# Second block's heads: granules split ahead of x's low halves, token sums dealt among query matmuls, turns among compressed keys

## The chip, the core and the metric

The kernel runs on one core of a Trainium2 chip. The metric is the device time of one execution in microseconds. The core has five engines that run their own instruction queues and meet at semaphores: TensorE (PE, with its weight loads PEld), VectorE (DVE), ScalarE (ACT), GpSimd (POOL) and SyncE (SP), which issues the transfers.

## What is computed

Two blocks of two layers each act on x, 512 tokens by 1024 features, in fp32. The first block (a gated MLP, a retention and a delta-rule branch) isn't touched by the change. The second block reads, cut to what matters:

```python
x = rms_norm(x, final_norm_g)                # final norm of the first block
mem_n = _rmsnorm(mem, mem_norm)              # 256 memory rows
for i in range(2):
    h = _rmsnorm(x, norm_mix[i])
    proj = h @ w_in[i]                       # i = 0: c_q (384), c_kv (256), k_pe (64), q_mem (512)
    mix = mla(proj) if i == 0 else gqa(proj)
    kv = mem_n @ w_mem_kv[i]                 # memory keys and values
    k = _rmsnorm(kv[:, :, 0], memk_norm)
    mem_out = attention(_rmsnorm(q_mem), k, kv[:, :, 1])
    x = x + concat(mix, mem_out) @ w_out[i]
    x = x + swiglu(_rmsnorm(x, norm_ffn[i]))
```

In mla, c_q and c_kv ("compressed" queries, keys and values) are normalised per token and multiplied by further weights. A norm needs a sum of squares over features for each token.

## The kernel before

**Products in three passes.** Each fp32 product is three reduced-precision ones (`three`, L838 to L841): high x high, low x high, high x low. So activations and weights each exist as a high part (a rounding cast on ScalarE) and a low part (a subtraction on GpSimd; for some on VectorE). Weights come in granules of 128 x 1024 through four slots: SyncE loads `raw`, ScalarE casts `wh` (`hi2`), GpSimd subtracts into `wl` (`lo2`, `split`, L2405, two halves of 512 columns). `hi2(g)` and `lo2(g)` treat the granule four places behind g: `split_granules("mk", [3])` makes the low half of the fourth granule of mv. A slot is cast anew when TensorE has finished the granule in it.

**Groups.** `attention_plan` lists the dense products at a layer's head. Layer 0: mk (memory keys, 4 granules), cq (queries with the shared key kpe, 448 columns, 4), mv (memory values, 4), ckv (compressed keys, 256 columns, 2), qm (memory queries, 4), and so on. Layer 1: mk, mv, qm, kv and so on. `dense` runs a group: all granules but the last two go granule by granule over the tiles of 128 tokens; the last two go tile by tile, so that tiles finish one after the other. With `mix`, one turn stands behind each tile.

**Turns.** `turn` transposes a finished, normalised tile back (L1437) into bank 6 or 7 in alternation, and ScalarE (`feature`, L2168) takes it out; for cq and ckv VectorE also takes a low part from the bank (`lows`, L3147). A bank is free when both have been.

**Statistics.** `statistics` on TensorE sums squares over the partitions, with ones as a one-column moving operand (`token_sums`, L843 to L849): two transposes of gains (L1474), then sums of msum (memory, 2 columns), in layer 0 also of ssum and of the last square (4 each), and of ssb (4), which VectorE adds up from eight squares made on ScalarE (`square_b` L2069, `add_b` L3139). The signal "summed" starts VectorE's and ScalarE's roots, with which GpSimd scales the tokens (`scale_tokens`, L2571).

**Layer 1's x.** VectorE makes ht (`scale_x`, L3132) in four buffers, ScalarE casts it to hh (`scaled_hi`, L2061), GpSimd makes hl = ht - hh (`scaled_lo`, L2552) and so frees the buffer: ht of k = 4 waits for hl of k = 0. VectorE's own order there is scale_x 0..3, add_b 1, scale_x 4, 5, add_b 2, scale_x 6, add_b 3, scale_x 7, add_b 4..7. ScalarE's is:

```python
cast("mk", [0, 1]); scaled_hi(0..1); cast("mk", [2]); scaled_hi(2..3); square_b(0..1)
cast("mk", [3]); take(to_token, "mk"); square_b(2); scaled_hi(4); cast("mv", [0])
scaled_hi(5); square_b(3); scaled_hi(6..7); cast("mv", [1]); square_b(4..7)
memory_values(); cast("mv", [2, 3]); take_root("mx"), ...
```

All orders are written out by hand; each engine takes its queue strictly in that order.

Of the kernel before, what the change touches and what calls it, by code (L numbers as in the profile page):

```python
# [22 lines left out]
P = 128  # L23
# [3 lines left out]
NT = T // P  # L27
# [266 lines left out]
N2_ADDED = {0: 0, 2: 7, 3: 13, 4: 20}  # L294
# [56 lines left out]
X0_TURN = 9  # L351
QUERY_TURNS = ((("qA", 0), ("qA", 1)), (("qA", 2), ("qA", 3)), (("qpe0", 0), ("qpe0", 1)), ())
QB_TURNS = (4, 6, 8, 9)
FILL_STEPS = (0, 1, 2, 3, 4, 6, 8, 10, 12, 14, 16, 18)


# [97 lines left out]
def build(nc, stream, params, consts, consts2, gains, xin, memin, out, n_granules):  # L454
# [43 lines left out]
    mv = sb("mv", [P, 4, 2])  # L498
# [120 lines left out]
    for i in range(2):  # L619
        def tiles_at(n, count, at, shape=(P, T), dt=F32):  # L620
            return [sb(f"{n}_{i}_{t}", list(shape), dt, at=at + t * int(np.prod(shape[1:])) * 4) for t in range(count)]
        b = BUF[i]
# [110 lines left out]
    def bc(ap, shape):  # L733
        return ap.broadcast_to(shape)
# [7 lines left out]
    with block:  # L742
# [92 lines left out]
        def _(pe):  # L835
# [7 lines left out]
            def token_sums(o, sq, one, start, stop):  # L843

                w = one.shape[1]
                for t in range(sq.shape[1] // P):
                    m = mm(o[:, t * w:(t + 1) * w], sq[:, t * P:(t + 1) * P], one, start=start and t == 0, stop=stop,  # L849
                           skip_group_check=True)  # L850
                return m
# [485 lines left out]
            def attention_block(i):  # L1337
                b, t = BUF[i], t2[i]
                done = []

                def dense(name, parts, free, mix=None):

                    grp = GROUPS[i][name]
                    hi_, lo_ = {"h": (hh, hl), "m": (b["mh"], b["ml"]), "cq": (b.get("cqh"), b.get("cql")),
                                "ckv": (b.get("ckvh"), b.get("ckvl"))}[grp.src]
                    if grp.src == "m":
                        pe.wait_ge(ms["lo"].sem, ms["lo"].at(i + 1, 2))
                    if grp.src in ("cq", "ckv"):
                        turns = count_before(TURNS[i], grp.src) + dict(TURNS[i])[grp.src]
                        pe.wait_ge(t["feat"].sem, t["feat"].at(turns))  # L1350
                        pe.wait_ge(t["feat_lo"].sem, t["feat_lo"].at(3 if grp.src == "cq" else 5))
                    n = len(grp.granules)

                    def piece(q, x):

                        g = ATT0[i] + grp.g0 + q
                        w = g % SLOTS
                        pe.wait_ge(lo_ready, g + 1)
                        if q == 0:
                            free(x)  # L1360
                        for k, at in grp.granules[q]:
                            if grp.src == "h" and x == 0:
                                if i == 0:
                                    pe.wait_ge(s["xl_ready"].sem, s["xl_ready"].at(DEPTH, k + 1))
                                else:
                                    pe.wait_ge(n2["lo"], N2_SCALED[3] + k + 1)
                            r = slice(x * P, (x + 1) * P)
                            o = three(bk[grp.banks[x]][:, 0:grp.width], hi_[:, k, r], lo_[:, k, r],
                                      wh[w][:, at:at + grp.width], wl[w][:, at:at + grp.width], k == 0, k == grp.nk - 1)
                        if q == n - 1 and x < grp.tiles - 1:  # L1370
                            o.then_inc(t["tile_done"].sem, 1)
                        if x == grp.tiles - 1:
                            o.then_inc(granule_done, 1)

                    if parts == "tile":
                        return piece
                    for q in parts:
                        if q < n - 2:
                            for x in range(grp.tiles):
                                piece(q, x)  # L1380
                    if n - 1 in parts:
                        for x in range(grp.tiles):
                            for q in range(max(0, n - 2), n):
                                piece(q, x)
                            if mix and x < len(mix):
                                for a in mix[x] if name == "qB" and i == 0 else [mix[x]]:
                                    turn(*a)

                def whole(name, free, mix=None):
                    dense(name, range(len(GROUPS[i][name].granules)), free, mix)  # L1390
# [7 lines left out]
                def evacuated(name):  # L1398
                    return lambda x: taken(name, x)
# [64 lines left out]
                def turn_all(name):  # L1464
                    for a in turns(name):
                        turn(*a)

                def statistics():

                    pe.wait_ge(n2["added"], N2_ADDED[3 * i] + 7)  # L1470
                    keys = ("q_pe", "k_pe") if i == 0 else ("gqa_q", "gqa_k")
                    for x, key in enumerate(keys):
                        g = gain[:, GAIN[key]:GAIN[key] + 1]
                        nc.tensor.transpose(bk[7][:, (x + 1) * P:(x + 2) * P], bc(g, [P, P]), C2["ident"])  # L1474
                    pe.wait_ge(ms["red"].sem, ms["red"].at(i + 1, 1))
                    token_sums(bk[7], b["msum"][:, :], C2["ones"][:, 0:1], True, True)
                    if i == 0:
                        pe.wait_ge(s["sq_added"].sem, s["sq_added"].at(DEPTH, 6))
                        token_sums(bk[7][:, 384:], ssum[:, :], C2["ones"][:, 0:1], True, False)
                        pe.wait_ge(s["sq_ready"].sem, s["sq_ready"].at(DEPTH, 8))  # L1480
                        token_sums(bk[7][:, 384:], sq2[3][:, :], C2["ones"][:, 0:1], False, True)
                    token_sums(bk[7][:, 392:], ssb[:, :], C2["ones"][:, 0:1], True, True).then_inc(n2["summed"], 1)

                def fill_bank(tiles, before):

# [2 lines left out]

                if i == 0:
                    whole("mk", merged_taken)  # L1490
                    dense("cq", range(2), x_taken)
                    statistics()
                    dense("cq", range(2, 4), None)
                    whole("mv", evacuated("mk"))
                    turn_all("mk")
                    turn_all("cq")
                    whole("ckv", evacuated("cq"))
                    turn_all("kpe")
                    dense("qm", range(1), evacuated("ckv"))
                    pe.wait_ge(t["rr"].sem, t["rr"].at(root_index(i, "x0") + 1))  # L1500
# [20 lines left out]
                else:  # L1521
                    whole("mk", down_taken(4))
                    whole("mv", down_taken(0))
                    down_taken(7)(0)
                    statistics()
                    dense("qm", range(2), lambda x: taken("mv", x) if x < 2 else down_taken(0)(x))
                    dense("qm", range(2, 4), None, turns("mk"))
                    dense("kv", range(2), evacuated("qm"))
# [203 lines left out]
        def _(act):  # L1732
# [321 lines left out]
            def attention_block(i):  # L2054
# [115 lines left out]
                def features(name):  # L2170
                    for x in range(dict(TURNS[i])[name]):
                        feature(name, x)
# [8 lines left out]
                if i == 0:  # L2181
# [16 lines left out]
                    take_root("cq")  # L2198
                    memory_values()
                    features("mk")  # L2200
                    features("cq")
                    cast("mv", [2, 3])
                    take(to_token, "ckv")
                    features("kpe")
                    cast("ckv", [0, 1])
                    take_root("ckv")
# [193 lines left out]
        def _(pool):  # L2400
# [141 lines left out]
            def attention_block(i):  # L2542
# [30 lines left out]
                if i == 0:  # L2573
                    split_granules("mk", range(4))
                    split_granules("cq", range(4))
                    scale_tokens("mk")
                    scale_tokens("cq")
                    split_granules("mv", range(4))
                    split_granules("ckv", [0])
                    scale_tokens("ckv")  # L2580
                    split_granules("ckv", [1])
                    split_granules("qm", range(4))
                    split_granules("kA", [0])
                    scale_tokens("kA")
                    for name in ("vA", "kB"):
                        split_granules(name, [0])
                    scale_tokens("kB")
                    split_granules("vB", [0])
                    split_granules("qpe", [0, 1])
                    scale_tokens("qpe0")  # L2590
                    scale_tokens("qpe1")
                    split_granules("qA", [0, 1])
                    split_granules("qB", [0, 1])
                else:
                    split_granules("mk", [0, 1, 2])
                    for k in range(4):
                        scaled_lo(k)
                    split_granules("mk", [3])
                    split_granules("mv", [0])
                    for k in range(4, KD):  # L2600
                        scaled_lo(k)
                    split_granules("mv", [1, 2, 3])
                    scale_tokens("mk")
                    split_granules("qm", range(4))
                    split_granules("kv", range(4))
                    scale_tokens("kv")
                    split_granules("qA", range(4))
                    split_granules("qB", range(4))
# [934 lines left out]
```

## Time and profile before

| | us |
|---|---|
| median of 3 runs | 2619.16 (2618.93 to 2619.23) |
| profiled execution, whole | 2619.03 |
| its span, first to last instruction | 2617.2 |
| PE busy | 2560.6 (98%) |
| DVE busy | 1035.6 (40%) |
| ACT busy | 1070.2 (41%) |
| POOL busy | 1327.5 (51%) |
| mean granted TensorE clock | 0.995 |

Rows name the engine, the line of the kernel, the operation and its tiles; in a timeline the first number is the start and the second the duration, both in us from the start of the span, and a bracket gives the idle time before it and what ended it. Matmuls are pipelined: their spacing counts, not their duration. Layer 0's head lies from 1257 to 1360 us, layer 1's from 1959 to 2060.

### The profile page before, as it was taken

How to read it: one execution, taken by the hardware profiler on the slowest of the kernel's cores; microseconds unless marked ns; L12 is line 12 of the kernel's file. 1: busy time of each engine (PE TensorE's matmuls, PEld its weight loads, DVE VectorE, ACT ScalarE, POOL GpSimd, SP SyncE). 2: the span in 40 equal slices, each digit the busy share in tenths (PEclk: the TensorE clock that was granted, in tenths of full speed). 3: DMA queues.
4: the chain of work that ended last, by engine and by line, in shares of the span. 5: the costliest groups of instructions: out<-in, count | busy, mean ns of one | idle time of the engine just before them, and what ended most of it. 6: DMA issues, size and time to landing. Idle time of an engine off the chain costs nothing.

```text
span 2617.2 us, 36454 instructions
## 1 busy us (share of the span) xinstructions
PE 2560.6 (98%) x12788; PEld 2053.4 (78%) x12788; DVE 1035.6 (40%) x2185; ACT 1070.2 (41%) x1648; POOL 1327.5 (51%) x1016
## 2 busy tenths in 40 slices
PE   9999999999999999999999999999999989999999
PEld 7878878888778787888876468888887746888887
DVE  6567442115575653113656632111015584211100
ACT  6336443334526444323546433333234463333321
POOL 6424655567633665556652125666557212566653
PEclk9999999999999999999999999999999999999999
DMA  5212112323221211333331113323333101233332
GB/s 197 83 48 82 48 34 89 96 98 130 81 65 65 66 41 57 97 96 113 105 97 33 33 42 96 96 96 96 96 106 119 57 25 49 90 96 98 96 103 72
DMA packets 62360, 215.03 MB, mean 82 GB/s; under 512 B 7312, under 2 KB 10512, under 8 KB 61840
## 3 DMA queue, kind: packets, MB, share of 16 engines
q1 hardware_dynamic: 62224, 213.28, 25.6%
q8 instruction: 78, 1.28, 0.2%
q14 instruction: 58, 0.48, 0.1%
HBM read 211.16 MB, written 2.10 MB: 81 GB/s over the span
## 4 chain that ended last, share of the span: by engine, by line
PE 62%; DVE 3%; ACT 1%; issue 1%; POOL 0%; DVEq 0%; ACTq 0%
PE bank L839 16%; PE bank L841 16%; PE bank L840 16%; PE pair L1624 2%; PE pair L839 2%; PE pair L840 1%; PE pair L841 1%; PE bank L1583 1%; PE bank L1584 1%; PE bank L1606 1%; PE pair L1437 1%; DVE soft L3326 1%; PE pair L849 0%; PE bank L1581 0%; PE bank L1199 0%
## 5 line engine op out<-in xcount | busy, mean ns | idle before, releaser
L2405 POOL TENSOR_TENSOR wl<-raw,wh 128x512 fp32r<-128x512 f32 x766 | 1021.7, 1357 | 1163.3 <-ACT wh L2036 381.9
L839 PE MATMUL bank<-hh,wh 128*128 128x512 f32 x1584 | 624.7, 394 | 2.3 <-DVE y L2907 2.3
L841 PE MATMUL bank<-hh,wl 128*128 128x512 f32 x1584 | 616.9, 389 | 0.0
L840 PE MATMUL bank<-hl,wh 128*128 128x512 f32 x1584 | 616.6, 389 | 0.0
L839 PEld LDWEIGHTS bank<-hh,wh 128*128 128x128 f32 x1584 | 297.5, 188 | 62.9 <-issue 3.2
L841 PEld LDWEIGHTS bank<-hh,wl 128*128 128x128 f32 x1584 | 297.3, 188 | 62.6
L840 PEld LDWEIGHTS bank<-hl,wh 128*128 128x128 f32 x1584 | 297.6, 188 | 59.9 <-issue 0.5
L2356 ACT CAST wh<-raw 128x1024 fp32r<-128x1024 f32 x120 | 125.5, 1048 | 254.0 <-PE pair L841 140.2
L1794 ACT CAST wh<-raw 128x1024 fp32r<-128x1024 f32 x104 | 109.1, 1050 | 128.8 <-PE bank L841 96.1
L839 PE MATMUL bank<-wh,hh 128*128 128x512 f32 (+2 forms) x352 | 139.8, 397 | 2.7 <-ACT vg L1813 1.6
L2036 ACT CAST wh<-raw 128x1024 fp32r<-128x1024 f32 x84 | 86.9, 1048 | 127.0 <-PE bank L841 107.6
L841 PE MATMUL bank<-wh,hl 128*128 128x512 f32 (+2 forms) x352 | 134.1, 381 | 0.0
L840 PE MATMUL bank<-wl,hh 128*128 128x512 f32 (+2 forms) x352 | 134.0, 381 | 0.0
L2995 DVE TENSOR_TENSOR gs<-gs,bank 128x512 f32<-128x512 f32 x24 | 16.4, 684 | 286.3 <-PE bank L841 286.3
L3369 DVE TENSOR_TENSOR at<-row,bank 128x512 f32<-128x512 f32 x44 | 30.3, 688 | 202.2 <-PE bank L841 199.4
L1989 ACT CAST wh<-raw 128x1024 fp32r<-128x1024 f32 x72 | 75.2, 1045 | 85.1 <-PE pair L841 43.8
L839 PE MATMUL bank<-ah,wh 128*128 (+1 forms) x264 | 102.7, 389 | 0.0
L840 PE MATMUL bank<-al,wh 128*128 (+1 forms) x264 | 102.7, 389 | 0.0
L841 PE MATMUL bank<-ah,wl 128*128 (+1 forms) x264 | 102.7, 389 | 0.0
L2005 ACT ACTIVATE gs<-bank 128x512 f32<-128x512 f32 x48 | 28.8, 600 | 166.5 <-PE bank L841 166.5
L3366 DVE TENSOR_TENSOR at<-row,bank 128x512 f32<-128x512 f32 x44 | 30.3, 688 | 162.7 <-PE bank L841 162.1
L839 PEld LDWEIGHTS bank<-wh,hh 128*128 128x128 f32 x352 | 66.9, 190 | 16.6 <-ACT vg L1813 3.5
(466 smaller groups left out, 4695.6 us busy)
## 6 DMA issues: line engine op xcount, KB each, us to landing
raw<-stream SPq DMA_DIRECT2D x384, 512.0 KB, 3.5
mraw<-memin SPq DMA_DIRECT2D x3, 1024.0 KB, 6.1
par<-params SPq DMA_DIRECT2D x2, 1124.5 KB, 8.7
out<-xT SPq DMA_DIRECT2D x8, 256.0 KB, 2.0
con<-consts SPq DMA_DIRECT2D x1, 1540.0 KB, 15.1
xT<-xin SPq DMA_DIRECT2D x2, 512.0 KB, 4.8
xT<-xin SPq DMA_DIRECT2D x1, 1024.0 KB, 8.6
con<-consts SPq DMA_DIRECT2D x1, 512.0 KB, 3.0
```

The lines of the kernel that those rows point to most:

```text
L839: mm(o, ah, bh, start=start, stop=False)
L840: mm(o, ah, bl, start=False, stop=False)
L841: return mm(o, al, bh, start=False, stop=stop)
L1624: x = mm(bk[value_bank(i, phase, a)], vv, pts[a % 2][kb][:, :], start=(kb == 0), stop=(kb == nk - 1))
L1794: nc.scalar.copy(wh[g % SLOTS][:, :], raw[g % SLOTS][:, :]).then_inc(hi_ready, 1)
L1989: nc.scalar.copy(wh[g % SLOTS][:, :], raw[g % SLOTS][:, :]).then_inc(hi_ready, 1)
L2005: A(gs[e][:, :], bk[e], ACT.Sigmoid).then_inc(s["gate_taken"].sem, 1)
L2036: nc.scalar.copy(wh[g % SLOTS][:, :], raw[g % SLOTS][:, :]).then_inc(hi_ready, 1)
L2356: nc.scalar.copy(wh[slot][:, :], raw[slot][:, :]).then_inc(hi_ready, 1)
L2405: m = TT(wl[slot][:, c], raw[slot][:, c], wh[slot][:, c].bitcast(F32), ALU.subtract)
L3366: V.tensor_tensor(at_[j][:, :], row[:, :], bk[2 * j], ALU.mult).then_inc(t["f_gate"].sem, 1)
L3369: V.tensor_tensor(at_[j][:, :], row[:, :], bk[2 * j + 1], ALU.mult).then_inc(t["f_up"].sem, 1)
```

## The change

It has three parts. (1) In layer 0 the token sums become a generator, and two of its one-column steps follow each k of cq's second granule; the wait for ssb moves behind the other sums. (2) In layer 0 the three turns of cq stand behind ckv's tiles 0 to 2 in place of standing ahead of ckv; ScalarE's order follows. (3) In layer 1 GpSimd splits mk's fourth part before any low half of x, mv's first part after two of them and mv's second after four.

```diff
+CKV_TURNS = ((("cq", 0),), (("cq", 1),), (("cq", 2),), ())
...
-                def dense(name, parts, free, mix=None):
+                def dense(name, parts, free, mix=None, weave=()):
...
                             o = three(bk[grp.banks[x]][:, 0:grp.width], hi_[:, k, r], lo_[:, k, r],
                                       wh[w][:, at:at + grp.width], wl[w][:, at:at + grp.width], k == 0, k == grp.nk - 1)
+                            for _ in zip(range(2), weave):
+                                pass
...
-                                for a in mix[x] if name == "qB" and i == 0 else [mix[x]]:
+                                for a in mix[x] if name in ("ckv", "qB") and i == 0 else [mix[x]]:
...
+                def column_sums(o, sq, start, stop):
+
+                    for c in range(sq.shape[1] // P):
+                        yield mm(o[:, c:c + 1], sq[:, c * P:(c + 1) * P], C2["ones"][:, 0:1], start=start and c == 0, stop=stop,
+                                 skip_group_check=True)
...
                 def statistics():
 
-                    pe.wait_ge(n2["added"], N2_ADDED[3 * i] + 7)
+                    if i:
+                        pe.wait_ge(n2["added"], N2_ADDED[3 * i] + 7)
...
-                        token_sums(bk[7][:, 384:], sq2[3][:, :], C2["ones"][:, 0:1], False, True)
-                    token_sums(bk[7][:, 392:], ssb[:, :], C2["ones"][:, 0:1], True, True).then_inc(n2["summed"], 1)
+                        yield from column_sums(bk[7][:, 384:], sq2[3][:, :], False, True)
+                        pe.wait_ge(n2["added"], N2_ADDED[0] + 7)
+                    m = None
+                    for m in column_sums(bk[7][:, 392:], ssb[:, :], True, True):
+                        if m is not None:
+                            yield m
+                    m.then_inc(n2["summed"], 1)
...
                     whole("mk", merged_taken)
-                    dense("cq", range(2), x_taken)
-                    statistics()
+                    dense("cq", range(1), x_taken)
+                    sums = statistics()
+                    dense("cq", range(1, 2), None, None, sums)
+                    for _ in sums:
+                        pass
                     dense("cq", range(2, 4), None)
                     whole("mv", evacuated("mk"))
                     turn_all("mk")
-                    turn_all("cq")
-                    whole("ckv", evacuated("cq"))
+                    whole("ckv", evacuated("cq"), CKV_TURNS)
...
                     features("mk")
-                    features("cq")
                     cast("mv", [2, 3])
-                    take(to_token, "ckv")
+                    for x in range(NT):
+                        to_token("ckv", x)
+                        for a in CKV_TURNS[x]:
+                            feature(*a)
...
-                    split_granules("mk", [0, 1, 2])
-                    for k in range(4):
+                    split_granules("mk", range(4))
+                    for k in range(2):
                         scaled_lo(k)
-                    split_granules("mk", [3])
                     split_granules("mv", [0])
+                    for k in range(2, 4):
+                        scaled_lo(k)
+                    split_granules("mv", [1])
                     for k in range(4, KD):
                         scaled_lo(k)
-                    split_granules("mv", [1, 2, 3])
+                    split_granules("mv", [2, 3])
```

## Rows read from the trace of the kernel before

**Rows 1.** Part 1 of the page: busy time by engine.
```profile
PE 2560.6 (98%) x12788; PEld 2053.4 (78%) x12788; DVE 1035.6 (40%) x2185; ACT 1070.2 (41%) x1648; POOL 1327.5 (51%) x1016
```
**Rows 2.** Timeline of PE, layer 1's mv and token sums.
```profile
1977.16 0.39 PE L841 MATMUL bank<-wh,ml 128*128 128x512 f32 x1
1981.12 0.80 PE L839 MATMUL bank<-wh,mh 128*128 128x512 f32 x1 [3.56 <-POOL wl L2405]
1981.71 0.63 PE L840 MATMUL bank<-wl,mh 128*128 128x512 f32 x1
...
1986.72 0.38 PE L1474 MATMUL pair<-con,gain 128*128 128x128 f32 x2
...
1988.20 0.49 PE L839 MATMUL bank<-wh,hh 128*128 128x512 f32 x1
```
**Rows 3.** Timeline of POOL, layer 1: low halves of x (hl) and splits (wl).
```profile
1973.12 5.48 POOL L2552 TENSOR_TENSOR hl<-ht,hh 128x512 fp32r<-128x512 f32 x4
1978.57 4.97 POOL L2405 TENSOR_TENSOR wl<-raw,wh 128x512 fp32r<-128x512 f32 x4
1983.51 5.01 POOL L2552 TENSOR_TENSOR hl<-ht,hh 128x512 fp32r<-128x512 f32 x4
```
**Rows 4.** Timeline of ACT, layer 1: casts and squares.
```profile
1972.53 1.03 ACT L2036 CAST wh<-raw 128x1024 fp32r<-128x1024 f32 x1
...
1975.75 0.62 ACT L2061 CAST hh<-ht 128x512 fp32r<-128x512 f32 x1 [0.69 <-DVE ht L3132]
1976.28 1.05 ACT L2036 CAST wh<-raw 128x1024 fp32r<-128x1024 f32 x1
...
1980.31 1.04 ACT L2036 CAST wh<-raw 128x1024 fp32r<-128x1024 f32 x1
1981.26 2.19 ACT L2069 ACTIVATE sqb<-xT 128x512 f32<-128x512 f32 x4
```
**Rows 5.** Busy time by stretch: span, PE, PEld, DVE, ACT, POOL, granted clock, DMA.
```profile
1277.50:1281.00 3.50, 3.50 (x30) 3.36 (x28) 0.00 (x0) 2.17 (x2) 2.53 (x3) 1.00 0.73 190
1281.00:1287.00 6.00, 6.00 (x21) 5.52 (x21) 4.03 (x32) 0.36 (x2) 1.42 (x2) 0.50 0.43 153
1304.90:1308.30 3.40, 2.49 (x15) 1.64 (x14) 1.76 (x2) 2.03 (x5) 3.40 (x4) 1.00 0.01 5
1308.30:1311.70 3.40, 2.18 (x19) 1.97 (x20) 1.41 (x2) 1.94 (x4) 3.40 (x4) 1.00 0.18 42
...
1981.00:1983.00 2.00, 1.89 (x5) 1.50 (x6) 0.98 (x2) 2.00 (x5) 2.00 (x3) 0.50 0.44 78
```
**Rows 6.** Timeline of PE, layer 0: token sums and cq.
```profile
1278.56 0.38 PE L1474 MATMUL pair<-con,gain 128*128 128x128 f32 x2
...
1280.93 1.82 PE L849 MATMUL pair<-con,ssb 128*128 128x1 f32 x8
1282.60 0.72 PE L839 MATMUL bank<-wh,hh 128*128 128x448 f32 x1
...
1287.90 0.36 PE L841 MATMUL bank<-wh,hl 128*128 128x448 f32 x1
...
1294.79 0.40 PE L839 MATMUL bank<-wh,mh 128*128 128x512 f32 x1
```
**Rows 7.** Timeline of PE, layer 0: turns and ckv's start.
```profile
1305.91 0.60 PE L1437 MATMUL pair<-con,tok 128*128 128x128 f32 x4
...
1308.22 1.06 PE L1437 MATMUL pair<-con,tok 128*128 128x128 f32 x8 [0.29 <-ACT mk L2168]
1310.50 0.63 PE L1437 MATMUL pair<-con,tok 128*128 128x128 f32 x4 [1.22 <-DVE cql L3147]
1310.89 0.36 PE L839 MATMUL bank<-wh,hh 128*128 128x256 f32 x1
...
1312.39 0.38 PE L839 MATMUL bank<-wh,hh 128*128 128x256 f32 x1
```
**Rows 8.** Timeline of POOL, layer 0: ckv's two splits.
```profile
1307.34 4.99 POOL L2405 TENSOR_TENSOR wl<-raw,wh 128x512 fp32r<-128x512 f32 x4
```
**Rows 9.** Timeline of PE, layer 1: mk's turns among qm's tiles.
```profile
2003.21 0.44 PE L1437 MATMUL pair<-con,tok 128*128 128x128 f32 x2 [1.11 <-POOL tok L2571]
...
2006.26 0.38 PE L1437 MATMUL pair<-con,tok 128*128 128x128 f32 x2
2006.40 0.48 PE L839 MATMUL bank<-wh,hh 128*128 128x512 f32 x1
2006.71 0.39 PE L840 MATMUL bank<-wl,hh 128*128 128x512 f32 x1
```
**Rows 10.** Timeline of DVE, layer 1: ht of k = 4 and ssb.
```profile
1974.97 0.75 DVE L3132 SCALAR_TENSOR_TENSOR ht<-xT,gain,pair 128x512 f32<-128x512 f32 x1 [1.25 <-POOL hl L2552]
...
1984.33 0.69 DVE L3139 TENSOR_TENSOR ssb<-pair,sqb 128x512 f32<-128x512 f32 x1
```

More of the change, by code:

```diff
@@ L1473, in statistics @@
                         g = gain[:, GAIN[key]:GAIN[key] + 1]
-                        nc.tensor.transpose(bk[7][:, (x + 1) * P:(x + 2) * P], bc(g, [P, P]), C2["ident"])
+                        yield nc.tensor.transpose(bk[7][:, (x + 1) * P:(x + 2) * P], bc(g, [P, P]), C2["ident"])
                     pe.wait_ge(ms["red"].sem, ms["red"].at(i + 1, 1))
-                    token_sums(bk[7], b["msum"][:, :], C2["ones"][:, 0:1], True, True)
+                    yield from column_sums(bk[7], b["msum"][:, :], True, True)
                     if i == 0:
                         pe.wait_ge(s["sq_added"].sem, s["sq_added"].at(DEPTH, 6))
-                        token_sums(bk[7][:, 384:], ssum[:, :], C2["ones"][:, 0:1], True, False)
+                        yield from column_sums(bk[7][:, 384:], ssum[:, :], True, False)
                         pe.wait_ge(s["sq_ready"].sem, s["sq_ready"].at(DEPTH, 8))
-                        token_sums(bk[7][:, 384:], sq2[3][:, :], C2["ones"][:, 0:1], False, True)
-                    token_sums(bk[7][:, 392:], ssb[:, :], C2["ones"][:, 0:1], True, True).then_inc(n2["summed"], 1)
+                        yield from column_sums(bk[7][:, 384:], sq2[3][:, :], False, True)
[5 more added lines that the diff above has]
+                    m.then_inc(n2["summed"], 1)
                 def fill_bank(tiles, before):
@@ L1524, in attention_block @@
                     down_taken(7)(0)
-                    statistics()
+                    for _ in statistics():
+                        pass
                     dense("qm", range(2), lambda x: taken("mv", x) if x < 2 else down_taken(0)(x))
```

## Prediction

> **What bounds the kernel now.** I read the page first: TensorE is busy 98% of the span [rows 1], so time can come only from its few holes, from stretches at a lower clock and from its own instructions. Then I read the timeline of TensorE at the head of each of the second block's two layers, where the change lies, and the other engines' timelines there.
>
> Second layer: matmuls start 0.227 us apart; after the one at 1977.16 the next starts at 1981.12, having waited 3.56 us for GpSimd's low half of a weight granule [rows 2]. It is the last granule of mv (mk's four splits each serve the granule four places on, so "mk 3" is mv's last). GpSimd splits it from 1978.57 to 1981.09, behind four low halves of x that began at 1973.12 [rows 3], though its high half was cast by 1973.56 [rows 4]. The engine comes back at 0.43 us a matmul, the clock granted at 0.50 in that stretch [rows 2, 5]. The sums over tokens run from 1986.72 to 1988.20 [rows 2].
>
> First layer: the token sums are one cluster of 2 transposes and 28 one-column matmuls (14 sums of two each), 1278.56 to 1282.60; the last 8 take 1.67 us, and the first 15 dense matmuls of 448 columns behind them take until 1287.90, 0.353 each, against 0.203 at full clock (48 of them end the stretch at 1294.79) [rows 6]. The granted clock is 0.50 from 1281 to 1287 and 1.00 just before [rows 5]. Then 20 transposes (mk's 8, cq's 12) take 1305.91 to 1310.89, with idle stretches among them, and ckv's first tile stands at 1312.39 for its second granule [rows 7]: GpSimd splits ckv's two granules from 1307.34 to 1312.33 [rows 8]. The cq turns lie in the shadow of that split.
>
> **Part 1, sums dealt among a tile of queries (first layer).** Now two sums follow each triple of 448-column matmuls of cq's granule 1: 24 dense matmuls with 14 sums and 2 transposes among them. The trace has no one-column matmul between dense ones. The nearest row is two transposes and a dense matmul in 0.45 us, 2006.26 to 2006.71, so 0.22 for the two, 0.11 each [rows 9], the same as in the cluster. The bounds are zero if every weight load hides, and 0.16 if each of the eight switches also costs 0.1. I take 0.11: 30 x 0.112 = 3.4, no dearer because eight switches show only a few hundredths. The inputs are there: the last addition (ssb) ended near 1274.4, well before its sums. Now: 4.04 (cluster) + 12.19 (48 matmuls, partly slow) = 16.2 us from 1278.56 to 1294.79. After: 3.4 + 48 x 0.203 = 13.1, if the clock stays. **Gain 3.0 us** (2.2 to 4).
>
> That the clock stays: in any few microseconds the woven stretch is dense for over half of the time (0.61 of each 1.05 us). The clock stayed at 1.00 over 1304.9 to 1311.7, where TensorE was busy 69% of the time and mostly with short transposes [rows 5]; it fell after 2.4 us of one-column matmuls alone.
>
> The Trainium skill ("TensorE: Matmul & The Clock Gate", "Step-by-step: what each phase is for") says the next tile's weights load while this tile's matmul runs. By that one load of every four short matmuls would hide behind a dense one, and part 1 would gain some 0.9 us more (8 x 0.11). Rows 9 show two full prices for two transposes, so no such hiding, and the sum goes without it.
>
> **Part 2, cq's turns among ckv's tiles (first layer).** Everything on ScalarE and GpSimd here follows TensorE's cq tiles, so GpSimd's ckv splits also come 3 us sooner, ending near 1309.4. TensorE ends mv near 1302.9, does mk's turns (until 1304.8, paced by ScalarE's copies) and then waits about 2.1 us for ckv's first granule and 1 us for its second. The turns that used to fill that hole are now behind it: 12 x 0.11 = **1.35 us lost**, with three switches up to 1.5. No wait goes in exchange; cq's waits for the ring of two banks (0.29 and 1.22 us [rows 7]) were in the shadow too. ScalarE gets mv's casts earlier by the two features it no longer does first, which nobody waits for. Between 1302.9 and 1309.4 TensorE now has 8 transposes and 12 matmuls of 256 columns, much less than in the held stretch above, so the clock may fall: 0 to 2 us, 0.4 taken. Net of the first layer: -3.0 + 1.4 + 0.4 = **-1.2 us** (-3 to +1.5).
>
> **Part 3, order of splits on GpSimd (second layer).** The work is the same; what changes is who is late.
> Gone: mv's last granule is split from 1973.64 (cast plus 0.08) to 1976.15, and TensorE needs it at 1977.39. So mv ends at 1977.39 + 18 x 0.227 = 1981.5 instead of 1986.72.
> Next late: TensorE then waits for the sum ssb (the "added" count in front of statistics). That sum hangs on GpSimd in a roundabout way. There are only four buffers ht2, so VectorE makes ht for k = 4..7 only when hl of k = 0..3 is done; ScalarE, strictly in order, casts hh 4, granule mv 0, hh 5, squares one part, casts hh 6, hh 7, granule mv 1, and only then squares the last four parts that ssb adds. Step by step with before's durations (split 2.5, hl 1.25 to 1.3 [rows 3]; ht 0.75 [rows 10]; hh to next cast 0.53, cast 1.05 [rows 4]):
> - hl 0 from 1976.15 to 1977.4 (before: 1973.12); ht 4 at 1977.5, before at 1974.97 [rows 10]; hl 1 until 1978.65; hh 4 at 1978.3, cast of mv 0 from 1978.8 to 1979.9.
> - GpSimd, which now has mv 0 ahead of hl 2, waits for that cast: split 1979.95 to 1982.45 (before, hl 2 and 3 were done by then: all four ended at 1978.6 [rows 3]).
> - hl 2 until 1983.7, hl 3 until 1984.95; ht 7 at 1985.1 to 1985.85; hh 7 at 1985.9; cast of mv 1 at 1986.4, before at 1980.31 [rows 4].
> - Squares begin 0.95 later, before at 1981.26 [rows 4], and ssb ended 3.76 after that (1984.33 + 0.69 [rows 10]): now 1986.4 + 0.95 + 3.76 = 1991.1.
> So statistics begin near 1991.2, 4.5 us after 1986.72, and TensorE has stood 9.7 us in one piece. **+4.5 us.**
> Clock: after 3.56 us of standing it came back at half [rows 2, 5], so it will here. The 14 sums and transposes then cost 0.209 each as in rows 6 (1.67 for 8): 2.9 instead of 1.48, **+1.4**. The dense matmuls behind them stay at half for 3 us (as from 1981.12 to 1984) to 5.3 us (the first layer, after a like cluster [rows 6]): 1.3 to 2.5 lost, **+1.8** taken.
> Given back: mk's turns come at 2003.21 after 1.11 us of waiting for GpSimd's scaling [rows 9], a chain that starts when the sums are done and takes 15.0 us from 1988.20. Now TensorE needs 1.8 + 60 x 0.227 = 15.4 us from the same point, so the wait goes: **-1.3**.
> Later splits (qm's) are ready at 1982.5, 1990, 1997.6 and 2000.1, each before TensorE, which starts qm near 1994.1 and needs the last two after 2006. They cost nothing.
> Sum: 4.5 + 1.4 + 1.8 - 1.3 = **+6.4 us** (5 to 8).
>
> **Sum.** -1.2 + 6.4 = +5.2 us. The profiled execution took 2619.03 for a span of 2617.2, 1.8 us lying around it unchanged; the median of the runs, 2619.16, agrees within 0.13. So 2619.2 + 5.2 = 2624.4 us. Nothing in the rest of the program is touched, and what follows each layer's head is fed by TensorE's own order, so the shifts should reach the end.
>
> **Rivals.** A change within 0.2% (5.24 us) is about what a measurement of this kernel can't tell from none.
> - *Forecast*: ssb is late in the second layer. 2621 to 2628, of which the part above 2624.4 counts as slower. Chance 0.78 in all, 0.42 above that line and 0.36 below it.
> - *ssb isn't late* (faster). If the squares don't wait for GpSimd's low halves, statistics start at ssb's present end, 1985.1: 1.6 us sooner than now, with 3.6 us of standing, and the scaling chain moves along. With the first layer at its best (-3) and a milder clock dip (-1), that is -5.6: 2613.5; with the first layer at -1.2 it is -2.8: 2616.3. It decides at hl 0: ht 4 must start at 1974.97 as before. Against it: GpSimd's own order and the four buffers. Chance 0.12, half of it past -0.2%.
> - *The weave drops the clock* (slower). If the one-column matmuls count like those in the cluster, the woven 9 us and some 3 us behind them run at half, and the first layer gives +2 to +3 instead of -1.2: 2628. Against it: over half of the stretch is dense. Chance 0.10.
> Slower 0.52, within 0.42, faster 0.06. The range holds the forecast with its bounds and reaches for the rivals to 2618.5 and 2628.5.
>
> **What would show it.** Right: the wait of TensorE on GpSimd's split of wl near 1977 gone, and one of 8 to 10 us in front of the second layer's gain transposes, released by VectorE's addition; GpSimd idle about 1 us before mv 0's split and 2.5 before mv 1's; the granted clock at half around and behind it; mk's turns there without a wait. In the first layer no clock dip at cq, a wait of 2 us and one of 1 us for ckv's splits, and 12 transposes behind them. Wrong: an addition ssb that ends by 1986 (then the rival holds), or a dip in the clock across cq.

## The result: 8 us slower, nearly all of it in the second layer

The changed kernel takes 2626.88 us (median of 8 runs, 2625.74 to 2627.38) against 2618.89 us before (8 runs in the same place, 2618.17 to 2619.59): 8.0 us more, ratio 1.0031 with a 95% interval of 1.002 to 1.0041. Its profiled execution took 2625.88 us with a span of 2624.1 us, 6.9 more than the span of before.

TensorE's busy time is nearly what it was, 2563.0 against 2560.6 [rows 1]: 2.4 us of the span's 6.9 are busy time, in part matmuls at a lower clock, and 4.5 are idle time. The first part of the page of the changed kernel:

```profile
PE 2563.0 (98%) x12788; PEld 2056.2 (78%) x12788; DVE 1033.6 (39%) x2185; ACT 1070.0 (41%) x1648; POOL 1326.4 (51%) x1016
```

The waits of TensorE in the changed kernel, 1950 to 2050 us (who waited on whom, us in total, times, longest):

```profile
PE pair L1484 <- DVE ssb L3161: 9.6, 1, 9.6
PE bank L840 <- DVE xT L3398: 0.9, 1, 0.9
```

The wait for GpSimd's split and the one for mk's scaled tokens are gone; one of 9.6 us on VectorE's sum ssb stands in their place. Where it comes from is read on the other engines of the second layer. This layer begins at 1960.10 in the changed trace and at 1959.61 in the one before, so 0.49 is to be taken off each time when the two are compared. First TensorE, then GpSimd, ScalarE and VectorE of the changed kernel:

```profile
1991.73 0.66 PE L1484 MATMUL pair<-con,gain 128*128 128x128 f32 x2 [9.59 <-DVE ssb L3161]
1992.19 0.85 PE L1474 MATMUL pair<-con,msum 128*128 128x1 f32 x4
1992.90 1.84 PE L1474 MATMUL pair<-con,ssb 128*128 128x1 f32 x8
```

```profile
1974.16 2.55 POOL L2425 TENSOR_TENSOR wl<-raw,wh 128x512 fp32r<-128x512 f32 x2 [0.48 <-ACT wh L2054]
1976.66 2.54 POOL L2572 TENSOR_TENSOR hl<-ht,hh 128x512 fp32r<-128x512 f32 x2
1980.48 2.52 POOL L2425 TENSOR_TENSOR wl<-raw,wh 128x512 fp32r<-128x512 f32 x2 [1.27 <-ACT wh L2054]
1982.96 2.49 POOL L2572 TENSOR_TENSOR hl<-ht,hh 128x512 fp32r<-128x512 f32 x2
1988.00 2.51 POOL L2425 TENSOR_TENSOR wl<-raw,wh 128x512 fp32r<-128x512 f32 x2 [2.55 <-ACT wh L2054]
```

```profile
1978.83 0.62 ACT L2079 CAST hh<-ht 128x512 fp32r<-128x512 f32 x1 [3.26 <-DVE ht L3154]
1979.36 1.05 ACT L2054 CAST wh<-raw 128x1024 fp32r<-128x1024 f32 x1
...
1986.88 1.04 ACT L2054 CAST wh<-raw 128x1024 fp32r<-128x1024 f32 x1
1987.83 2.18 ACT L2087 ACTIVATE sqb<-xT 128x512 f32<-128x512 f32 x4
```

```profile
1978.05 0.75 DVE L3154 SCALAR_TENSOR_TENSOR ht<-xT,gain,pair 128x512 f32<-128x512 f32 x1 [3.81 <-POOL hl L2572]
...
1990.89 0.69 DVE L3161 TENSOR_TENSOR ssb<-pair,sqb 128x512 f32<-128x512 f32 x1
```

mv's last split is done before TensorE needs it, but hl 0 starts at 1976.66 (before 1973.12 [rows 3]), so ht 4 comes at 1978.05 (1974.97 [rows 10]). GpSimd then waits 1.27 us for mv 0's cast and 2.55 us for mv 1's, for which ScalarE itself had been waiting on ht. The last four squares begin at 1987.83 (1981.26 [rows 4]), and ssb with them. The sums over tokens run at half clock, 1991.73 to 1994.61, 2.88 us where it was 1.48 [rows 2]. The dense matmuls behind them run at half clock until 1999.4. So mk's turns come 50.5 us after the layer's start (2010.61), before 43.6 (2003.21 [rows 9]): +6.9 us by then, of which 4.5 is the later start of the sums, 1.4 the sums themselves and 1.0 what follows them.

In the first layer the changed trace nets nothing. The stretch from cq's first matmul to kpe's turns is 1269.31 to 1322.99, 53.68 us, and was 1268.83 to 1322.55, 53.72. The sums gain 2.95 of it by mv's start, and the stretch from there to kpe's turns gives that back. TensorE there, and the granted clock by stretch (span, PE, PEld, DVE, ACT, POOL, clock, DMA), in the changed kernel:

```profile
1304.62 0.80 PE L1440 MATMUL pair<-con,tok 128*128 128x128 f32 x4 [0.62 <-ACT mk L2186]
1307.42 0.58 PE L840 MATMUL bank<-wh,hh 128*128 128x256 f32 x1 [2.00 <-POOL wl L2425]
```

```profile
1272.00:1283.00 11.00, 11.00 (x69) 10.40 (x68) 1.81 (x4) 3.82 (x5) 7.39 (x6) 1.00 0.61 192
1303.00:1307.00 4.00, 1.81 (x11) 1.03 (x9) 1.20 (x2) 3.23 (x7) 4.00 (x4) 0.95 0.01 4
1307.00:1311.00 4.00, 3.58 (x17) 3.58 (x17) 0.00 (x0) 0.81 (x1) 4.00 (x4) 0.50 0.46 136
```

The clock stays at 1.00 across the woven sums and falls to 0.50 behind the hole that the turns left, until about 1313.4.

### The profile page after: what moved, and what is told of

Same layout as the page of the kernel before. It is cut to its first block, busy times and chain, and to the rows that moved or that the text cites. A ratio compares the mean times of both kernels' runs of the same rounds, so it can differ in the third digit from the quotient of the medians.

```text
span 2624.1 us, 36454 instructions
## 1 busy us (share of the span) xinstructions
PE 2563.0 (98%) x12788; PEld 2056.2 (78%) x12788; DVE 1033.6 (39%) x2185; ACT 1070.0 (41%) x1648; POOL 1326.4 (51%) x1016
## 4 chain that ended last, share of the span: by engine, by line
PE 62%; DVE 3%; ACT 2%; issue 1%; POOL 1%; DVEq 0%; ACTq 0%
PE bank L840 16%; PE bank L842 16%; PE bank L841 16%; PE pair L1642 2%; PE pair L840 2%; PE pair L841 1%; PE pair L842 1%; PE bank L1601 1%; PE bank L1602 1%; PE bank L1624 1%; PE pair L1440 1%; DVE soft L3348 1%; POOL wl L2425 0%; PE bank L1599 0%; ACT wh L2054 0%
```

## The experiments

The kernel before ran beside each of them on the same chip. Medians of both and the interval of the ratio stand with each; a single execution of the kernel before varies from 2615.9 to 2620.7, so the traces and the medians are read together. Each states what it leaves changed.

**One part at a time.** `sums_only` keeps part 1 of the diff, `turns_only` part 2, `splits_only` part 3, `sums_and_turns` parts 1 and 2.

> Part 1 alone (token sums dealt among cq's second granule), the other two parts undone. Theory (the cluster's clock fall is the cost, woven sums keep the clock): 2.5 to 3.5 us faster than the kernel before, the granted clock at 1.00 from cq to mv, 56 one-column matmuls of the first layer unchanged in number. Rival (the woven sums gain nothing that reaches the end, since GpSimd's split of mv's last granules is next): 0 to 1 us.

Measured: 2616.75 against 2618.86, 2.1 us faster (ratio 0.9985 to 1.0003, so it isn't clear of none by the runs alone), a little under the 2.5 to 3.5 expected. The trace gives the mechanism: cq's start to mv's is 23.00 us against 25.96 before, 2.96 less, at full clock throughout:

```profile
1273.00:1295.00 22.00, 22.00 (x121) 20.10 (x121) 12.50 (x78) 8.77 (x14) 9.86 (x9) 1.00 0.36 114
```

TensorE in the woven stretch of the same kernel, one k of 3 dense matmuls and 4 one-column ones in 1.06 us, 0.36 for the four, which with the slower dense one behind them (0.29 instead of 0.20) makes 0.11 for each:

```profile
1276.03 0.46 PE L840 MATMUL bank<-wh,hh 128*128 128x448 f32 x1
1276.32 0.36 PE L841 MATMUL bank<-wl,hh 128*128 128x448 f32 x1
1276.52 0.37 PE L842 MATMUL bank<-wh,hl 128*128 128x448 f32 x1
1276.73 0.50 PE L1474 MATMUL pair<-con,ssum 128*128 128x1 f32 x4
1277.09 0.45 PE L840 MATMUL bank<-wh,hh 128*128 128x448 f32 x1
```

> Part 2 alone (cq's turns among ckv's tiles). Theory (the turns leave the shadow of ckv's split, and the emptied hole lets the clock fall): 2.5 to 3.5 us slower than before, clock at 0.50 somewhere between 1309 and 1317 us. Rival 1 (the clock holds, only the 12 transposes are exposed): 1.2 to 1.6 us slower. Rival 2 (the turns gain because their waits on the two banks go): faster.

Measured: 2620.08 against 2618.41, 1.7 us slower (0.9999 to 1.0017). In its trace the clock stays at 1.00 from 1303 to 1316, and the stretch from cq to kpe's turns is 55.02 us, 1.3 more than before: rival 1, the exposed transposes alone. The median lies between rival 1 and the theory, but its interval, from about none to 4.5 us slower, holds all of these. This profiled execution, 2618.53, is 1.5 us below the kernel's own median: in the second layer it reached mk's turns 41.7 us after the layer's start, the kernel before in 43.6, with the same orders on all engines there. The last section says where that came from.

> Parts 1 and 2, the order of splits undone. Theory (part 2 gives back what part 1 gains): within 0.7 us of before. Rival (the trace's clock fall at ckv was a chance of that execution): 1 to 1.7 us faster.

Measured: 2618.04 against 2618.41, 0.4 us faster (0.9991 to 1.0009): the theory by the median. In its trace, though, the hole in front of ckv is there and the clock does not fall; cq to kpe's turns is 52.05 us, 1.7 less than before. The waits of TensorE, 1300 to 1330 us, and the clock behind them:

```profile
PE bank L840 <- POOL wl L2425: 2.8, 2, 2.0
PE pair L1440 <- ACT mk L2186: 0.6, 1, 0.6
```

```profile
1307.00:1310.00 3.00, 1.70 (x12) 1.50 (x12) 0.00 (x0) 1.41 (x2) 3.00 (x3) 1.00 0.29 57
1310.00:1313.00 3.00, 2.49 (x21) 2.49 (x22) 0.00 (x0) 0.70 (x2) 3.00 (x4) 1.00 0.75 238
```

So behind a wait of 2.0 us in front of ckv the clock fell in the changed kernel and did not fall here. What decides it, these profiles don't show. The changed kernel has only one wait there, of 2.0 us: at half clock ckv's first tile takes so long that the second split, 0.8 us of waiting here, is done in time.

> Part 3 alone (order of GpSimd's splits in the second layer). Theory (hl late -> ht, hh, squares and ssb late -> statistics wait): 6.5 to 8 us slower than before, all of it between 1977 and 2010 us, with a wait of 9 to 10 us on ssb. Rival (the loss comes from the first layer or from several small shifts): under 4 us slower.

Measured: 2625.55 against 2618.86, 6.7 us slower (1.0018 to 1.0038), with the same wait of 9.6 us on ssb. From the layer's start to mk's turns it takes 49.65 us in place of 43.6, 6.05 more. Part 3 carries the loss; the three medians by part, -2.1 + 1.7 + 6.7, give +6.3 for the whole, within the interval of the change (5.2 to 10.7 us).

**What in the new order is slow.** `last_first` undoes part 3 but for one swap (against the kernel before):

```diff
-                    split_granules("mk", [0, 1, 2])
+                    split_granules("mk", range(4))
                     for k in range(4):
                         scaled_lo(k)
-                    split_granules("mk", [3])
                     split_granules("mv", [0])
```

> The kernel before with one swap on GpSimd in the second layer: mk's fourth split ahead of the four low halves of x, mv's splits left where they were. Theory (each low half is 3 us late but GpSimd no longer waits for mv 0's cast between them): ssb ends near 1987.4, statistics near 1987.5, standing of some 6 us, 1.5 to 4 us slower than before. Rival (the interleaving of mv 0 and mv 1 costs nothing, the 3 us at the head are all of it): as slow as part 3 alone, 6.5 us or more. Second rival (the split's wait was all): 4 us faster.

Measured: 2622.05 against 2618.41, 3.6 us slower (1.0005 to 1.0024), a wait of 6.1 us on ssb instead of 9.6:

```profile
PE pair L1483 <- DVE ssb L3153: 6.1, 1, 6.1
PE bank L840 <- DVE xT L3390: 0.9, 1, 0.9
```

GpSimd in this kernel no longer waits for a cast among the low halves of x:

```profile
1973.41 2.55 POOL L2420 TENSOR_TENSOR wl<-raw,wh 128x512 fp32r<-128x512 f32 x2 [0.47 <-ACT wh L2051]
1975.92 5.06 POOL L2567 TENSOR_TENSOR hl<-ht,hh 128x512 fp32r<-128x512 f32 x4
1980.93 2.50 POOL L2420 TENSOR_TENSOR wl<-raw,wh 128x512 fp32r<-128x512 f32 x2
```

Both halves of the new order cost: the split ahead of hl some 3.6 us, the splits of mv 0 and mv 1 between the low halves another 3.1. The length of the wait splits up, too. Counted from the layer's start, ssb ends at 25.4 us in the kernel before, 28.0 here and 31.5 in `splits_only`: 2.6 and 6.1 later. TensorE would have had to wait for it anyway: without the wait for the split it ends mv at 21.9, 3.5 before ssb's old end. 3.5 + 2.6 is the wait of 6.1 here, 3.5 + 6.1 the one of 9.6.

**Is it ssb's path?** In the second layer the squares and additions are pulled forward. ScalarE makes squares 0-1 after hh 1, 2-3 after hh 3 and 4-7 after mv 0's cast; VectorE adds five before ht 4 and the last two before ht 5; the ones that ht is multiplied with move to bank 3, so that the sums need not wait for the last ht (qm's fourth tile, which uses that bank, waits for it instead). ScalarE's order from mk's tokens on, against the kernel before:

```diff
                     take(to_token, "mk")
-                    square_b(2)
-                    scaled_hi(4)
                     cast("mv", [0])
-                    scaled_hi(5)
-                    square_b(3)
-                    for k in range(6, KD):
-                        scaled_hi(k)
-                    cast("mv", [1])
                     for n in range(4, KD):
                         square_b(n)
+                    scaled_hi(4)
+                    cast("mv", [1])
+                    for k in range(5, KD):
+                        scaled_hi(k)
```

`before_sums_early` has this with GpSimd's old order, `splits_sums_early` with the new one (parts 1 and 2 undone), `sums_splits_early` adds part 1.

> The kernel before with only the early squares and additions in the second layer, GpSimd's order as it was. Theory (there TensorE is held by mv's last split and ssb is ready in time either way): the wait of 3.6 us stays, time within 1 us of before. Rival (ssb's path already costs something in the kernel before): 1.5 us or more faster.

Measured: 2618.43 against 2618.86 (0.9989 to 1.0007), the wait on the split still 3.1 us. In the kernel before ssb isn't what TensorE waits for.

> Part 3 alone, and in the second layer ScalarE makes the eight squares and VectorE adds them before the low halves of x are needed (squares 0-1 after hh 1, 2-3 after hh 3, 4-7 after mv 0's cast; additions ahead of ht 5; the ones that ht is multiplied with lie in bank 3 in place of bank 7). The order on GpSimd is that of the changed kernel. Theory (only ssb's path makes the new order slow): no wait on ssb, statistics near 1981.5, no wait on mv's last split, 4 to 6 us faster than before. Rival (the new GpSimd order is bad in itself, by low halves or by qm's granules that come late): still 3 us or more slower than before.

Measured: 2617.62 against 2618.86, 1.2 us faster (0.9985 to 1.0003, not clear of none); 7.9 less than `splits_only`. No wait on ssb and none on the split, so ssb's path was the whole of part 3's loss. But the gain expected beyond that, 4 to 6 us, isn't there. The waits of TensorE from 1950 to 2050 us and VectorE's timeline show who took it:

```profile
PE bank L840 <- issue: 2.7, 1, 2.7
PE pair L1440 <- POOL tok L2593: 2.0, 1, 2.0
```

```profile
1986.01 8.81 DVE L3112 SCALAR_TENSOR_TENSOR rn<-mom 128x8 f32<-128x8 f32 x1
1994.85 0.17 DVE L3113 SCALAR_TENSOR_TENSOR rn<-mom,rn 128x8 f32<-128x8 f32 x1
```

qm may start only when ScalarE has taken mv out of its bank, which it did at 1983.79, behind hh 6 and 7, which wait for the late low halves. And an operation on 8 columns stands 8.81 us, until GpSimd ends a run of hl and wl at 1994.8; mk's scaling and turns hang on it. In this trace mk's turns came 43.65 us after the layer's start, as before: the whole head start was spent.

> Parts 1 and 3 with the early squares and additions, part 2 undone. Theory (the gains of the two heads add): 7 to 9 us faster than the kernel before. Rival (a wait behind qm takes the second layer's gain back): 3 to 4 us faster.

Measured: 2615.06 against 2618.41, 3.3 us faster (0.9979 to 0.9997): the rival, with the same 2.7 us in front of qm. Here mk's turns (1999.55) wait for nothing, 41.4 us after the layer's start: the operation that stood 8.81 us above takes 1.35 in this trace, with the same order on GpSimd.

**The two waits that took the gain.** `values_early` is `sums_splits_early` with ScalarE's `memory_values()` moved from behind hh 7 to behind hh 5. `moments_psum` is the kernel before with one operand of the small VectorE operations in bank 7, for which the eight operations that make the moments run twice; `values_early_psum` has both:

```diff
+                    far = (i, name) == (1, "mk")
+                    mm_ = bk[7][:, 400:416].rearrange("p (x f) -> p x f", f=2) if far else mom
...
-                    own(V.scalar_tensor_tensor(r, mom[:, 0:j, 0], scale, mom[:, 0:j, 0], ALU.mult, ALU.mult))
+                    own(V.scalar_tensor_tensor(r, mm_[:, 0:j, 0], scale, mom[:, 0:j, 0], ALU.mult, ALU.mult))
```

> The kernel before, with one thing changed in the second layer: the moments of the memory keys are also written to the spare columns of bank 7, so that each of the three small VectorE operations behind them reads one operand from there instead of both from SBUF. Theory (a VectorE operation with two SBUF inputs stands while GpSimd works through its splits; the 4.80 us of the first one is that): the operation takes about 0.2 us, mk's turns come without a wait, 1 to 1.5 us faster than before. Rival (the 4.80 us is something else, such as the own semaphore): it stays, no difference.

Measured: 2618.46 against 2618.71 (0.999 to 1.0008). The operation takes 0.17 us in its trace, the next two too, while GpSimd is at its splits, and the wait in front of mk's turns is gone:

```profile
1990.36 0.17 DVE L3108 SCALAR_TENSOR_TENSOR rn<-pair,mom 128x8 f32<-128x8 f32 x1
1990.56 0.17 DVE L3110 SCALAR_TENSOR_TENSOR pair<-pair,rn 128x8 f32<-128x8 f32 x1
1990.77 0.16 DVE L3121 SCALAR_TENSOR_TENSOR rn<-em,pair 128x8 f32<-128x8 f32 x1
```

The mechanism holds, and not on this trace alone. In the eleven profiles with both operands in SBUF the three operations together took 2.59 to 9.15 us; in the two with one operand in bank 7 they took 0.50.

The gain of 1 to 1.5 us doesn't show in the median. The traces say why little was to be had: with GpSimd's old order TensorE's wait in front of mk's turns is 1.11 us in the kernel before, 0.90 in `before_sums_early`, 0.58 in `turns_only` and none in `sums_only` and `sums_and_turns`, 0.5 on average, and the interval of the ratio spans some 2.4 us to either side. The profiled execution flatters the kernel: it is the fastest of its 11 (2615.67), and 1.4 of the 2.6 us by which it reached mk's turns sooner than the kernel before came from the clock, which stayed at 1.00 behind the wait for the split.

> Parts 1 and 3 with early squares, and ScalarE takes mv out of its banks ahead of hh 6 and 7. Theory (the wait in front of qm was ScalarE's order; but the scaling chain of mk still ends late): qm starts 2.7 us sooner, mk's turns come at the same time, so the time stays within 1 us of 2615, about 3 to 4 us faster than before. Rival (qm's start is what counts): 6 to 7 us faster.

Measured: 2611.07 (8 runs) against 2618.71, **7.6 us faster** (0.9962 to 0.9983). This beats both kernels. The rival was right: qm's start counted.

```profile
PE bank L840 <- DVE xT L3406: 0.9, 1, 0.9
PE bank L840 <- POOL wl L2432: 0.7, 1, 0.7
PE pair L1440 <- POOL tok L2598: 0.3, 1, 0.3
```

The sums run at 1979.09, 21.9 us after the layer's start (before 27.1), and mk's turns at 1995.87, 38.7 after it (before 43.6).

> The last kernel with the moments of the memory keys in bank 7 as well. Theory: with the small operations free, mk is scaled right behind the last split, its turns wait under 1 us, and both heads' gains add: 6 to 8 us faster than before. Rival: GpSimd's splits end too late for it (the scaling stands behind them in the queue), 3 to 5 us faster.

Measured: 2611.40 against 2618.71, 7.3 us faster (0.9963 to 0.9983), no different from `values_early`. GpSimd's scaling starts at once behind the splits in both (1994.02 here, 1993.76 there): there the roots were ready in time anyway. So the size was as expected, the reason given for it wasn't: the operand in bank 7 added nothing.

## Why the prediction was right, step by step

The forecast was 2624.4 us, slower; 2626.9 was measured, within the range and 2.5 above the forecast.

*Part 3, the path to ssb*: right in mechanism and in nearly every time. Less 0.49, the changed trace has hl 0 at 1976.17 (forecast 1976.15), mv 0's split at 1979.99 (1979.95), mv 1's cast at 1986.39 (1986.4), the statistics at 1991.24 (1991.2). The sums cost 2.88 us (2.9). Dense matmuls at half clock cost 2.4 us in the changed trace and 1.5 in `splits_only` (1.8), taken as the time from qm's first matmul to mk's turns (16.0 and 15.15) less 60 x 0.227. By the same count the kernel before has 1.4 there, 1.27 of it the hole in front of mk's turns (1.3 in the forecast); that hole went, as said. Sum: +6.9 us in the changed trace, +6.05 in that of `splits_only` and +6.7 by its medians, against +6.4.

*Part 1*: 3.0 forecast, 2.96 in the trace, 2.1 by the medians, whose interval includes 3. The price of 0.11 per woven matmul held, and the clock stayed. The Trainium skill ("TensorE: Matmul & The Clock Gate", "Step-by-step: what each phase is for") has the next tile's weights load while this tile's matmul runs. The saving that the prediction derived from it isn't there: 1.06 us for each k is the full price, and 0.95 would be that with one hidden load. Two numbers of the prediction were off here without a consequence. Between 1282.60 and 1287.90 lie 14 dense matmuls and not 15 [rows 6], 0.379 each. And 0 to 0.16 for each woven matmul gives a gain of 1.7 to 6.5, not 2.2 to 4.

*Part 2*: 1.35 us exposed, 1.3 measured in the trace of `turns_only`. The term that was mis-sized is the clock behind the emptied hole: 0.4 us was taken, and the changed kernel's trace shows 1.6 (53.68 against 52.05 in `sums_and_turns`), since 6 us of ckv ran at 0.50. The bounds (0 to 2) held it. The wait of 1 us for ckv's second split, also forecast, came in `turns_only` and `sums_and_turns` (0.8), where the clock held; in the changed kernel the slow matmuls took its place, so 1.6 is what remains after that saving. That either can happen behind the same hole was in the forecast only as the width of these bounds.

*The 2.5 us* between forecast and median: 1.2 from the first layer, nearly all of it the clock at ckv, and 0.5 from the second in the trace; the changed kernel's profiled execution was itself 1.0 below its median, and the median of the kernel before was 0.3 lower here than the one that the forecast started from. What the other executions have more, no profile shows.

*The rivals*: "ssb isn't late" falls with the 9.6 us wait. "The weave drops the clock" falls with the clock of 1.00 from 1272 to 1283. Its price was too low: 9 and 3 us at half clock lose 6 us, which makes -1.2 into +4.8 for the first layer, not +2 to +3, and a time above the range.

*What the forecasts of the experiments missed*: 4 to 6 us for `splits_sums_early`. Its step said that statistics at 1981.5 would carry through; overlooked was that ScalarE's copy of mv stands behind hh 7. `sums_splits_early` was then expected 7 to 9 us faster on the same ground. For `values_early` I trusted that mk's chain would end at a fixed time; the trace of `sums_splits_early` shows mk's turns waiting for nothing, so they came sooner as soon as qm did. For `turns_only` I took from the changed kernel's one profile that the clock falls, which it didn't there. `moments_psum` was expected to gain what one profile of the kernel before showed as a wait.

## What to carry to other kernels

Before moving a step ahead in a queue, follow what is pushed back through every ring of buffers and every in-order queue to the first sum or norm that the bound engine waits for; here three splits of 2.5 us made ssb 6.1 us late through four buffers and ScalarE's order. Ask also what the bound engine waits for next: in the kernel before ssb ended 3.5 us after the time at which mv ends without its wait, so even with no delay 3.5 of the 5.2 us gained there would have been waited away. Work that stands in the shadow of another engine's step is free where it is, and moving it among dense work makes it cost its full time. When a wait goes and the time doesn't, look at the next two waits in the trace of that very kernel: the gain of 7.6 us, 2 to 3 of it part 1's, needed the squares, and then one copy, moved ahead. And a wait that stands in one profile need not be in the median: look at the same stretch in the profiles of several kernels.

## What the hardware showed that was not expected

A VectorE operation on 128 x 8 elements with both inputs in SBUF took from 0.17 to 8.81 us while GpSimd worked on SBUF. There are two patterns. In six of the eleven profiles it stood once and long, 2.38, 3.33, 3.59, 4.60, 4.80 and 8.81 us, each time until GpSimd ended its run of operations, and the two behind it took 0.17 each. In the other five it took 0.17 to 1.35 and the two behind it 1.2 each, and GpSimd's run went on behind the first two. Which of the two comes isn't settled by the order of the work: `splits_sums_early` and `sums_splits_early` have the same orders in this layer and show 8.81 and 1.35. With one operand in PSUM all three took 0.16 or 0.17, in both profiles. The Trainium skill ("SBUF — State Buffer", "Who interferes with whom") says that a VectorE operation with two SBUF inputs contends with a GpSimd operation that reads SBUF, that the lock on the port pair they share is exclusive, and that with one SBUF input at most, outside the 2-port modes, there is no contention. The last agrees with the 0.17 us. A GpSimd instruction is 1.26 us here, which fits the stands of 1.2 us, but 8.81 us is seven of them, so a single instruction is no bound.

The clock of TensorE isn't the same behind the same hole. Behind 2 us of waiting in the first layer it fell to 0.50 in the changed kernel and stayed at 1.00 in `sums_and_turns` and `turns_only`. Behind the wait of 3.56 us for mv's split in the second layer, which all kernels with GpSimd's old order and the old squares have, it stayed at 1.00 in `turns_only` and `moments_psum`, was at 0.50 for 2.7 us in the kernel before and for 5 to 6 in `sums_only` and `sums_and_turns`. The token sums began 25.7 to 28.6 us after the layer's start by that alone. Behind 6.1 and 9.6 us of waiting it was 0.50 in all three profiles. `turns_only`, then `sums_only`:

```profile
1982.80:1986.90 4.10, 4.10 (x18) 3.38 (x19) 2.79 (x4) 2.78 (x6) 4.10 (x4) 1.00 0.61 155
1978.80:1983.80 5.00, 5.00 (x12) 3.94 (x13) 2.79 (x4) 2.87 (x6) 5.00 (x5) 0.50 0.58 172
```

A single profile doesn't price such a hole.
